# The gate row of a mixture of experts multiplied into each expert's output, and the residual state used as accumulator

## The reference, cut to what matters

```
logits  = xt @ router                                  # 256 x 8
top_w   = softmax of the two largest logits; gates = 256 x 8, two non-zero per token
out     = sum over e of gates[:, e] * ((silu(xt @ w1[e]) * (xt @ w3[e])) @ w2[e])    # e = 0..7
h       = h + row * out            # row: 1024 numbers from the adaLN product, "the gate row" here
```

## Time and profile before

| | |
|---|---|
| median of 3 runs | 1843.59 us (1837.85 to 1845.21) |
| profiled execution, whole time | 1843.83 us |
| its span, first to last instruction | 1842.0 us |
| TensorE busy | 1688.1 us, 92% |
| VectorE busy | 1260.6 us, 68% |
| ScalarE busy | 824.7 us, 45% |
| GpSimd busy | 143.7 us, 8% |
| stretch of experts 3 and 4 up to `y` (1110 to 1215 us), VectorE | 93.1 of 105 us |
| the same, TensorE | 102.9 of 105 us |

### The profile page before, as it was taken

One profiled execution on the slowest core, in us unless ns is written; L12 is line 12 of the kernel. 1 busy time (PEld: TensorE's weight loads), 2 busy tenths in 40 slices (PEclk: granted clock), 3 DMA queues, 4 the chain that ended last, 5 costly groups with the idle time before them and its releaser, 6 DMA issues. The chain is left out here.

```text
span 1842.0 us, 21595 instructions
## 1 busy us (share of the span) xinstructions
PE 1688.1 (92%) x8734; PEld 1435.9 (78%) x8734; DVE 1260.6 (68%) x1712; ACT 824.7 (45%) x987; POOL 143.7 (8%) x134
## 2 busy tenths in 40 slices
PE   5987979899999998899879999999979989889998
PEld 2766867788788886798668888887869868779986
DVE  6566884577755544776668898889886576566643
ACT  6342332422212324233366776777745444445532
POOL 2320001100110021320100000000020000000000
PEclk9997998999999999898969999999998999789999
DMA  8323342255655432212249889898956522144553
GB/s 332 99 107 114 121 146 77 103 198 202 240 214 197 160 139 74 69 47 69 72 151 347 319 329 353 295 351 301 358 204 213 191 81 94 56 154 166 185 198 114
DMA packets 59063, 333.58 MB, mean 181 GB/s; under 512 B 14530, under 2 KB 14849, under 8 KB 25680
## 3 DMA queue, kind: packets, MB, share of 16 engines
q1 hardware_dynamic: 56080, 321.54, 47.5%
q10 hardware_dynamic: 1728, 6.54, 1.0%
q0 software_dynamic: 1152, 4.08, 0.7%
HBM read 331.00 MB, written 1.13 MB: 180 GB/s over the span
## 5 line engine op out<-in xcount | busy, mean ns | idle before, releaser
L2043 DVE TENSOR_TENSOR wlo__65<-raw__64,whi__66 128x2048 fp32r<-128x2048 f32 (+3 forms) x64 | 144.9, 2264 | 84.7 <-ACT whi__66 L1512 84.7
L2043 DVE TENSOR_TENSOR wlo__61<-raw__60,whi__62 128x2048 fp32r<-128x2048 f32 (+2 forms) x64 | 145.3, 2270 | 66.6 <-ACT whi__62 L1512 66.6
L1512 ACT ACTIVATE whi__66<-raw__64 128x2048 fp32r<-128x2048 f32 (+3 forms) x64 | 115.3, 1802 | 99.5 <-DMA raw__64<-in_ffn_w 30.5
L1512 ACT ACTIVATE whi__62<-raw__60 128x2048 fp32r<-128x2048 f32 (+2 forms) x64 | 118.9, 1858 | 90.2 <-DMA raw__60<-in_ffn_w 43.5
L2043 DVE TENSOR_TENSOR wlo__69<-raw__68,whi__70 128x2048 fp32r<-128x2048 f32 (+4 forms) x50 | 109.3, 2185 | 30.7 <-ACT whi__70 L1512 30.7
L2076 DVE SCALAR_TENSOR_TENSOR wsum__71<-raw__68,silu_rows 128x1024 f32<-128x1024 f32 x84 | 100.0, 1220 | 6.6 <-DMA raw__68<-in_ada_w 6.0
L1512 ACT ACTIVATE whi__70<-raw__68 128x2048 fp32r<-128x2048 f32 (+4 forms) x50 | 90.4, 1808 | 15.2 <-DMA raw__68<-in_w_ff 11.8
L3140 POOL TENSOR_TENSOR keep__58<-keep__58,keep__59 128x1 f32<-128x1 f32 (+3 forms) x48 | 50.2, 1049 | 594.2 <-DVE keep__58 L2117 594.2
L2314 DVE TENSOR_REDUCE keep__58<-ps 128x1 f32<-128x256 f32 (+1 forms) x104 | 56.6, 544 | 17.6 <-PE ps L1153 12.3
L2043 DVE TENSOR_TENSOR wlo__233<-raw__232,whi__234 128x2048 fp32r<-128x2048 f32 (+1 forms) x24 | 50.7, 2112 | 11.4 <-ACT whi__234 L1512 11.4
L2043 DVE TENSOR_TENSOR wlo__229<-raw__228,whi__230 128x2048 fp32r<-128x2048 f32 (+1 forms) x24 | 52.8, 2199 | 0.3 <-ACT whi__230 L1512 0.2
(11 more groups left out here) (1142 smaller groups left out, 5367.2 us busy)
## 6 DMA issues: line engine op xcount, KB each, us to landing
raw__68<-in_ada_w SPq DMA_DIRECT2D x26, 1024.0 KB, 4.9
raw__68<-in_moe_w SPq DMA_DIRECT2D x24, 1024.0 KB, 5.3
raw__60<-in_moe_w SPq DMA_DIRECT2D x24, 1024.0 KB, 5.5
raw__64<-in_moe_w SPq DMA_DIRECT2D x16, 1024.0 KB, 5.3
raw__228<-in_moe_w SPq DMA_DIRECT2D x16, 1024.0 KB, 6.0
raw__232<-in_moe_w SPq DMA_DIRECT2D x16, 1024.0 KB, 6.6
raw__142<-in_ada_w SPq DMA_DIRECT2D x13, 1024.0 KB, 5.8
raw__64<-in_ffn_w SPq DMA_DIRECT2D x10, 1024.0 KB, 6.1
```

The costliest lines, as they stand in the source:

```text
L1512: e.activation(t.hi(), t.raw(), ACT.Copy).then_inc(*did("hi", i))
L2043: e.tensor_tensor(t.lo(), t.raw(), t.hi().bitcast(F32), ALU.subtract).then_inc(*did("lo", i))
```

## The change

`yg`: VectorE multiplies each half of `y` in its PSUM bank by the gate row, before ScalarE's and VectorE's copies. `MACC` is no longer turned into the state at the end: `acc` of expert 0 starts from `h`, that of expert 7 writes to `h`, the second round adds to `h`. GpSimd's `hgate` and `hpre` and VectorE's `moe_h` go. Who waited for `moe_h` waits for `acc` of expert 7, and in the `If` of the second round TensorE and ScalarE wait at its end for the last four `acc`.

In the order of the diff: the events, TensorE's and ScalarE's second round (the same in both), ScalarE's high copies, VectorE's `acc`, its products, its additions at the end, GpSimd's part.

```diff
+    def summed_up():
+        return [("acc", 1, 7, t, half) for t in range(2) for half in range(2)]
...
         if stage == "moe":
-            return [("moe_h", t)]
+            return [("acc", 0, 7, t, half) for half in range(2)]
...
+        def once_more(r):
+            experts(r)
+            for s, n in state["due"](*summed_up()):
+                e.wait_ge(s, n)
+        again(e, state, ask(e, state), once_more)
...
                 for half in range(2):
                     high("yph", (r, ex, half), YP[0][:, half * 512:half * 512 + 512], bank("y", r, ex, half),
-                         ("y", r, ex, 10), *xg_free(r, ex, "scat", 1, 1))
+                         ("yg", r, ex, half), *xg_free(r, ex, "scat", 1, 1))
...
-                    past = [("acc", r, ex - 1, t, half)] if ex else [("acc", 0, 7, t, half)] if r else []
-                    past = past + ([("hpre", t), *spr(11)] if (r, ex) == (0, 7) else [])
+                    h = h_t[t][:, half * 512:half * 512 + 512]
+                    past = [("acc", r, ex - 1, t, half)] if ex else [("acc", 0, 7, t, half)] if r else [("msq", t)]
...
-                    gates = GBC[:, D + half * 512:D + half * 512 + 512]
-                    if r:
-                        e.scalar_tensor_tensor(out=TR, in0=b, scalar=g, in1=gates, op0=ALU.mult, op1=ALU.mult).then_inc(*link())
-                        for s, n in linked():
-                            e.wait_ge(s, n)
-                        m = e.tensor_tensor(dst, dst, TR, ALU.add)
-                    elif ex == 7:
-                        m = e.scalar_tensor_tensor(out=dst, in0=b, scalar=g, in1=gates, op0=ALU.mult, op1=ALU.mult)
-                    elif ex == 0:
-                        m = e.tensor_scalar(dst, b, g, None, ALU.mult)
-                    else:
-                        m = e.scalar_tensor_tensor(out=dst, in0=b, scalar=g, in1=dst, op0=ALU.mult, op1=ALU.add)
-                    m.then_inc(*did("acc", r, ex, t, half))
+                    e.scalar_tensor_tensor(out=h if r or ex == 7 else dst, in0=b, scalar=g, in1=dst if ex and not r else h,
+                                           op0=ALU.mult, op1=ALU.add).then_inc(*did("acc", r, ex, t, half))
...
                  feed(("y", r, ex, 10))
                 for half in range(2):
+                    for s, n in due(("y", r, ex, 10), *spr(11)):
+                        e.wait_ge(s, n)
+                    yb = bank("y", r, ex, half)
+                    e.tensor_tensor(yb, yb, GBC[:, D + half * 512:D + half * 512 + 512], ALU.mult).then_inc(*did("yg", r, ex, half))
+                for half in range(2):
                     low("ypl", (r, ex, half), YP[1][:, hs], bank("y", r, ex, half), YP[0][:, hs], ("yph", r, ex, half))
...
-        for t in range(2):
-            for s, n in due(("acc", 1, 7, t, 0), ("acc", 1, 7, t, 1), ("hpre", t)):
-                e.wait_ge(s, n)
-            e.tensor_tensor(h_t[t], h_t[t], MACC[t], ALU.add).then_inc(*did("moe_h", t))
...
-        for t in range(2):
-            for s, n in due(("acc", 0, 6, t, 0), ("acc", 0, 6, t, 1), *spr(11)):
-                e.wait_ge(s, n)
-            e.tensor_tensor(MACC[t], MACC[t], GBC[:, D:2 * D], ALU.mult).then_inc(*did("hgate", t))
-            for s, n in due(("hgate", t)):
-                e.wait_ge(s, n)
-            e.tensor_tensor(h_t[t], h_t[t], MACC[t], ALU.add).then_inc(*did("hpre", t))
```

More of the change, by code:

```diff
@@ L148 @@
     "lam_v": ("tab", "lam_s", "lam_u"), "route_v": ("mdf", "sel", "mcnt"),
-    "moe_v": ("hot", "gxt_v", "xgl", "hmul", "htl", "acc", "ypl"), "moe_a": ("pt", "gxt_a", "xgh", "hsil", "hth", "yph"),
+    "moe_v": ("hot", "gxt_v", "xgl", "hmul", "htl", "yg", "acc", "ypl"), "moe_a": ("pt", "gxt_a", "xgh", "hsil", "hth", "yph"),
     "mix_v": ("srot", "sqk_v", "sv_v", "kps", "lms", "latn", "latc", "latl", "kper", "gcopy"),
@@ L424, in _build @@
     assert max(A3.col, M.col + 3 * 4096) <= CB0 + 2048 - 64 - NMOE
-    TR = cols("piece", CB0 + 2048 - 64 - NMOE - 512, 512)
-    assert M.col + 3 * 4096 <= CB0 + 2048 - 64 - NMOE - 512
     S = Region("mix", WORK)
@@ L1408, in tensor_program @@
         state["loads"] = (2, *slot_m)
-        again(e, state, ask(e, state), experts)
+        def once_more(r):
[3 more added lines that the diff above has]
+        again(e, state, ask(e, state), once_more)
         state["loads"] = None
@@ L1873, in scalar_program, with once_more @@
         experts(0)
-        again(e, at, at["taken"], experts)
+        def once_more(r):
+            experts(r)
+            for s, n in due(*summed_up()):
+                e.wait_ge(s, n)
+        again(e, at, at["taken"], once_more)
         feed(("scat", 1, 7, 1, 1))
@@ L1879, in scalar_program @@
         norm_turned("s", 0)
-        free = [("moe_h", t) for t in range(2)] + [("scat", 1, 7, 1, 1)]
+        free = summed_up() + [("scat", 1, 7, 1, 1)]
         for s, n in due(*free):
@@ L1886, in scalar_program @@
             *did("bg", by=16))
-        for s, n in due(("moe_h", 0), ("moe_h", 1)):
-            e.wait_ge(s, n)
         e.dma_start(MSK2, cst_d[:, DILM:DILM + 1536]).then_inc(*did("msk2", by=16))
@@ L2825, in scattered @@
                     g = GATE[:, t * 8 + ex:t * 8 + ex + 1]
-                    past = [("acc", r, ex - 1, t, half)] if ex else [("acc", 0, 7, t, half)] if r else []
-                    past = past + ([("hpre", t), *spr(11)] if (r, ex) == (0, 7) else [])
-                    if r and (ex, t, half) > (0, 0, 0):
-                        n = ex * 4 + t * 2 + half - 1
-                        past.append(("acc", 1, n // 4, n // 2 % 2, n % 2))
+                    h = h_t[t][:, half * 512:half * 512 + 512]
+                    past = [("acc", r, ex - 1, t, half)] if ex else [("acc", 0, 7, t, half)] if r else [("msq", t)]
                     for s, n in due(("scat", r, ex, t, half), ("sel",), ("mcnt",), *past):
                         e.wait_ge(s, n)
-                    gates = GBC[:, D + half * 512:D + half * 512 + 512]
-                    if r:
-                        e.scalar_tensor_tensor(out=TR, in0=b, scalar=g, in1=gates, op0=ALU.mult, op1=ALU.mult).then_inc(*link())
-                        for s, n in linked():
-                            e.wait_ge(s, n)
-                        m = e.tensor_tensor(dst, dst, TR, ALU.add)
-                    elif ex == 7:
-                        m = e.scalar_tensor_tensor(out=dst, in0=b, scalar=g, in1=gates, op0=ALU.mult, op1=ALU.mult)
-                    elif ex == 0:
-                        m = e.tensor_scalar(dst, b, g, None, ALU.mult)
-                    else:
-                        m = e.scalar_tensor_tensor(out=dst, in0=b, scalar=g, in1=dst, op0=ALU.mult, op1=ALU.add)
-                    m.then_inc(*did("acc", r, ex, t, half))
+                    e.scalar_tensor_tensor(out=h if r or ex == 7 else dst, in0=b, scalar=g, in1=dst if ex and not r else h,
+                                           op0=ALU.mult, op1=ALU.add).then_inc(*did("acc", r, ex, t, half))
                     empties(("scat", r, ex, t, half), ("acc", r, ex, t, half))
@@ L3230, in gpsimd_program @@
         for t in range(2):
-            for s, n in due(("acc", 0, 6, t, 0), ("acc", 0, 6, t, 1), *spr(11)):
-                e.wait_ge(s, n)
-            e.tensor_tensor(MACC[t], MACC[t], GBC[:, D:2 * D], ALU.mult).then_inc(*did("hgate", t))
-            for s, n in due(("hgate", t)):
-                e.wait_ge(s, n)
-            e.tensor_tensor(h_t[t], h_t[t], MACC[t], ALU.add).then_inc(*did("hpre", t))
-        for t in range(2):
             norm_rsqrt("s", t)
-        for s, n in due(("scat", 1, 7, 1, 1), ("moe_h", 0), ("moe_h", 1)):
+        for s, n in due(("scat", 1, 7, 1, 1), *summed_up()):
             e.wait_ge(s, n)
```

## The result

The changed kernel takes 1852.84 us in the median of 9 runs (1843.73 to 1858.34), the kernel before 1841.32 beside it (9 runs, 1834.11 to 1849.0). The ratio is 1.0059, 95% interval 1.0038 to 1.008: slower, by 11 us in the medians. The forecast was 1851 us in a range of 1839 to 1858. The profiled execution took 1852.84 us (span 1851.0) against 1843.83 (span 1842.0), 9.0 us more.

What follows compares the result with a forecast made beforehand. TensorE was taken as the bound, with 0.2 to 0.3 us slack at each expert's third tile. 13.2 - 4.9 - 1.6 + 0.5 = +7.2 us on the profiled 1843.83 gave 1851 us, 8-in-10 range 1839 to 1858.

Steps and rivals of the forecast that it cites:

- even joints, four: Passage from an even expert to the next: TensorE's third weight tile late by 2.0, 1.2, 1.5 and 1.5, together 6.2 us.
- odd joints, three: Passage after experts 1, 3 and 5, where VectorE comes late: third weight tile 2.3 us late each, 7.0 together.
- GpSimd's removal: Expert 7: without GpSimd's hgate and hpre, VectorE's splits are no longer slowed and TensorE needs 4.9 us less.
- end of the stage: After TensorE's last y: VectorE's two additions go (-2.27 us), first product and handover come (+0.72): -1.6 us.
- clock at the joints: TensorE's gaps after experts 1, 3 and 5 may lower the clock; none or one of three: +0.5, bounds 0 and +5.1 us.
- The price of a product in PSUM: One VectorE multiplication of 128x512 in PSUM: 0.68 us, taken from the low copies of y, bounds 0.60 and 1.22.
- The chain S + 0.72, + 1.69, + 3.63, + 6.1: From S, VectorE's first product: start of ScalarE's high copies, third tile's split, VectorE's part, TensorE's matmul, in us.
- The rival that counted only VectorE's time: Between experts: each passage costs 1.2 us of products minus 0.3 slack, 6.3 in all; 1844 us, chance 0.12.
- the rival with no gain there: Expert 7: the split is slow for another reason than GpSimd, so no gain; +12.1 us, 1856 us, chance 0.03.
- The splits gain no lead: Denies a rival: between experts splits run further ahead, 2.8 us lost after even experts; 1840 us, chance 0.15.
- which leaves the Else over 2 us: After the last y: ten of sixteen transposes, 2.3 us, precede VectorE's split end, leaving TensorE's Else over 2 us.
- The rival's three falls: After experts 1, 3 and 5 the clock falls each time, +5.1 us; total +11.8, 1856 us, chance 0.18.

Runs made afterwards that it cites:

- idle products: The kernel before, with two same-size VectorE multiplications per expert in SBUF at the product's place, for which nobody waits: 1848.09 us, ratio 1.0038.
- no product: The changed kernel without the two products per expert; ScalarE's copies wait for y, and the gate row is not in the result: 1834.91 us, ratio 0.9959.
- four ahead: The changed kernel with four weight tiles instead of two split ahead of the work on y, on ScalarE and VectorE: 1846.9 us, ratio 1.0022.
- four and three: The changed kernel with four tiles split ahead of the work on y on ScalarE and three on VectorE, instead of two: 1837.35 us, ratio 0.9987.
- the row in expert 7: Experts 0 to 6 as in the kernel before; VectorE does GpSimd's four state operations in expert 7, the only one with products: 1834.73 us, ratio 0.9956.
- the changed kernel again: The changed kernel itself, unedited, timed and profiled a second time against the kernel before: 1851.73 us, ratio 1.0046.
- three ahead on ScalarE: The changed kernel with three tiles instead of two split ahead of the copies on ScalarE alone, VectorE as it was: 1840.74 us, ratio 1.0012.
- three on both: The changed kernel with three tiles instead of two split ahead of the work on y, on ScalarE and VectorE: 1846.86 us, ratio 1.0025.

## Why the prediction was right

The forecast was +7.2 us on the profiled execution, measured +9.0, of which -1.1 lie outside the stage (+0.9 before it, -2.0 behind it). Within it, +7.2 were forecast and +10.0 came. In the medians the change cost 11.5 us, where 7.2 were forecast. That 1851 us lies within 2 us of the 1852.84 measured is in part luck: beside it the kernel before took 2.3 us less than in the runs that the forecast started from. The time lies just inside what was called "within 0.5%" (below 1853 us, chance 0.59), the ratio of 1.0059 just outside it.

| term | forecast | measured |
|---|---|---|
| even joints, four | 2.0, 1.2, 1.5, 1.5 | 1.39, 1.69, 2.12, 1.33 |
| odd joints, three | 2.3 each | 2.42, 2.41, 2.44 |
| joints in all | +13.2 | +13.8 |
| GpSimd's removal | -4.9 | -4.9 |
| end of the stage | -1.6 | -0.5 |
| clock at the joints | +0.5 | +1.5 |

- **The price of a product in PSUM** was 0.68 us, as taken from the low copies: 0.73 from the first product's start to ScalarE's copy. Writing the bank that it reads cost VectorE nothing more here: 1.29 us for two products, 1.28 for the two low copies.
- **The chain S + 0.72, + 1.69, + 3.63, + 6.1** came as + 0.73, + 1.82, + 3.76, + 6.15. The step that differs is ScalarE's two copies (1.09 from start to split, where 0.97 was taken), since the second now waits for the second product. The single even joints lie up to 0.6 us off their forecasts, because S moved: at 4 and 5 it is 1.44 us behind TensorE's first tile (1223.54 to 1224.98), where it was 0.95. There ScalarE stood 1.00 us for raw__68 to land, and 0.55 us for raw__60 behind it, so S hangs on the loads too, which the forecast did not look at. The sum of the even joints, 6.5 against 6.2, hardly differs.
- **That ScalarE's order is the larger part** was argued, and is shown now: VectorE's own time is 5.65 (idle products), and one split moved on ScalarE gives back the other 8. The rival that counted only VectorE's time underrates the joints by as much; its 6.3 was close to the 5.65. The Trainium skill's rule of first in, first out ("TensorE: Matmul & The Clock Gate", the array's architecture) is borne out: raw__64, issued at 1158.5 and landed 6.2 us later, stayed unsplit until 1175.63, behind a copy that waited 3.36 us.
- **GpSimd's removal** is -4.88 us in the change and -4.90 alone; the rival with no gain there is out.
- **The splits gain no lead.** S stayed where VectorE's backlog puts it at the odd joints (VectorE runs without a gap from 1169.40 to 1176.4 at 3 and 4), and at the even ones, where the splits of the first two tiles waited for their loads, the third tile was late by 1.3 to 2.1, not 0.7.
- **The step that failed is the end of the stage**, "which leaves the Else over 2 us": -1.6 us were forecast and -0.5 came. The transposes start 3.44 us behind the last scatter, and in five more traces without the additions 3.46 to 3.88 us (no product, four ahead, four and three, the row in expert 7, the changed kernel again), each time with TensorE's `Else` as the releaser. In the two with three tiles ahead on ScalarE it is 3.29 and 3.27 us, and VectorE's `Else` is named. Before, the additions hid all this: 4.76 us behind the last scatter. So the transposes are 0.14 us nearer to the end of y (8.74 us, where it was 8.88), not 1.6. VectorE lost the additions' 2.27 us and paid the product's 0.7, as forecast, but its own `Else` took 2.44 us instead of 2.14; its scaling began 2.61 us behind the start of the split instead of 2.07, since it stood 0.45 us for the transposes; and from there to the first matmul it is 3.50 us instead of 3.25, since ScalarE's scaling stood 1.25 us for them. 0.3 + 0.54 + 0.25 is the 1.1 us by which the term was off. The transposes are late in part because the scatters ran 0.45 us longer: the clock fell in them, behind the gap of 2.24 us that the product opened. No run takes an `Else` out, so its share of the 3.44 us is the profile's attribution and not shown by an experiment.
- **The clock** was under-sized: none or one fall of three was forecast, one and two were seen. The rival's three falls were not seen, but its +11.8 us was reached: the second profile shows +12.1 in the stage, with two falls.

The deciding comparison, 7.2 forecast and about 10 measured in the stage, is right in its mechanism and 2.8 us low, 2.1 of it in two small terms, the end of the stage and the clock. What is not explained is the 2.0 us behind the stage, beyond the clock that is seen there, and why the two profiles of the changed kernel differ by 0.9 us more at the joints than by a fall.

## What to carry to other kernels

When a step is put ahead of something that two engines read in turn, price the split or copy that stands *behind* the wait on the second engine, not the step: here 1.3 us of products cost 2.0 us a joint, and only 0.8 once ScalarE was one tile ahead of VectorE. Let the producer lead its consumer by one item across such a wait; moving both further ahead by the same number gave back only 2.1 and 2.9 of the 13.8 us here, and VectorE's hole moved to a later tile. And work that is to leave a slow engine belongs where the fast one is idle: four full-width operations in expert 7 cost nothing there, fourteen half-width ones at the joints cost 13.8 us.

## What the runs showed of the hardware

- An `If` that is not taken, with an `Else` that only brings semaphores up to date, is not free. In the eight traces without the additions TensorE's first instruction behind it came 3.27 to 3.88 us after the last scatter; VectorE stood 2.0 to 2.4 us there in all eleven, ScalarE 2.20 in the changed kernel. TensorE's was hidden before.
- A gap of 2.2 to 2.3 us on TensorE sometimes brought the clock from 2.4 to 1.2 GHz and sometimes not: behind three of the six odd joints of two profiles, and in the last scatters of three of the seven profiles that have a gap of 2.24 us there (the changed kernel once of twice, three ahead on ScalarE, three on both). It fell behind the gap of 2.40 us in the kernel with three ahead on both, too. One fall at a joint cost 1.5 us.
- VectorE and GpSimd on SBUF together slow each other: 4.49 instead of 2.28 us for a split of 128x2048; GpSimd's multiplications of 128x1024 took 2.41 us the first time and 4.45 the second.
